# Time mixing: small key, receptance and state products moved between and behind the large ones, one state sum per chunk, two state buffers

## The reference, cut to what matters

```python
xrkv = x[None] + xx[None] * mu[:3, None, None, :]
r, k, v = jnp.einsum('nbsd,nde->nbse', xrkv, w_rkv)
decay = jnp.exp(-jnp.exp(w_log.astype(f32)))
a = jax.nn.sigmoid(a0 + (xa @ a1) @ a2)
g = jax.nn.sigmoid(xg @ g1) @ g2
kk = kk / jnp.maximum(jnp.sqrt(jnp.sum(kk * kk, axis=-1, keepdims=True)), 1e-12)
k = k * (1 + (a - 1) * k_a)
bh = kk * ah

def step(state, inp):
    r_t, w_t, k_t, v_t, kk_t, b_t = inp
    sa = jnp.einsum('bhvk,bhk->bhv', state, -kk_t)
    state = (state * w_t[:, :, None, :] + sa[..., None] * b_t[:, :, None, :]
             + v_t[..., None] * k_t[:, :, None, :])
    return state, jnp.einsum('bhvk,bhk->bhv', state, r_t)
```

## Time and profile before

| | us |
|---|---|
| median of 3 runs | 1254.25 (1253.86 to 1259.63) |
| the profiled execution's own time | 1260.84 |
| its span | 1259.1 |
| PE busy | 1143.4 (91%) |
| DVE busy | 933.9 (74%) |
| ACT busy | 555.9 (44%) |
| mean granted PE clock | 0.943 |

### The profile page before, as it was taken

One profiled execution on the slowest core, in us unless ns is written; L12 is line 12 of the kernel. 1 busy time (PEld: TensorE's weight loads), 2 busy tenths in 40 slices (PEclk: granted clock), 3 DMA queues, 4 the chain that ended last, 5 costly groups with the idle time before them and its releaser, 6 DMA issues.

```text
span 1259.1 us, 20232 instructions
## 1 busy us (share of the span) xinstructions
PE 1143.4 (91%) x7950; PEld 914.9 (73%) x7950; DVE 933.9 (74%) x1242; ACT 555.9 (44%) x797; POOL 9.7 (1%) x27
## 2 busy tenths in 40 slices
PE   5899999898689999999999997888978877999998
PEld 1678888776467788877788885666758865888886
DVE  4888888688967988878888886887880876644453
ACT  2454444455844444355445435493232213543331
POOL 2000000000000000000000000000000000000000
PEclk8999999899799999999999998889976788999999
DMA  9889887373229789866888893125321112655540
GB/s 328 285 286 321 304 292 263 134 267 69 67 68 347 273 294 321 309 227 232 288 299 299 291 348 115 50 85 168 124 67 38 51 54 99 201 170 199 200 167 34
DMA packets 185852, 252.88 MB, mean 201 GB/s; under 512 B 30449, under 2 KB 121585, under 8 KB 185777
## 3 DMA queue, kind: packets, MB, share of 16 engines
q1 hardware_dynamic: 181554, 251.32, 59.0%
q10 hardware_dynamic: 4224, 0.52, 0.3%
HBM read 249.71 MB, written 2.10 MB: 200 GB/s over the span
## 4 chain that ended last, share of the span: by engine, by line
PE 69%; DVE 17%; DMA 5%; issue 4%; ACT 4%; SPq 0%; POOL 0%; DVEq 0%; ACTq 0%; POOLq 0%
PE bank L725 20%; PE bank L727 19%; PE bank L726 19%; DVE ada_acc L1839 4%; DVE gu_lo L1911 3%; DMA last_raw<-in_ffn_w_down_dram 2%; DVE dn_lo L1921 1%; DMA front<-in_ada_w_dram 1%; ACT gu_hi L1334 1%; PE bank L1200 1%; PE bank L787 1%; PE bank L1085 1%; DMA ada_raw<-in_ada_w_dram 1%; PE bank L734 1%; DVE probs L2453 1%
## 5 line engine op out<-in xcount | busy, mean ns | idle before, releaser
L725 PE MATMUL bank<-gu_hi,xT_hi 128*128 128x512 f32 (+1 forms) x944 | 375.4, 398 | 22.4 <-DVE gu_lo L1911 9.1
L726 PE MATMUL bank<-gu_lo,xT_hi 128*128 128x512 f32 (+1 forms) x944 | 371.9, 394 | 0.0
L727 PE MATMUL bank<-gu_hi,xT_lo 128*128 128x512 f32 (+1 forms) x944 | 371.7, 394 | 0.0
L1911 DVE TENSOR_TENSOR gu_lo<-raw,gu_hi 128x2048 fp32r<-128x2048 f32 (+1 forms) x108 | 239.8, 2252 | 15.3 <-ACT gu_hi L1334 14.9
L725 PEld LDWEIGHTS bank<-gu_hi,xT_hi 128*128 128x128 f32 x944 | 180.9, 192 | 66.5 <-issue 17.5
L726 PEld LDWEIGHTS bank<-gu_lo,xT_hi 128*128 128x128 f32 x944 | 180.8, 192 | 38.7 <-issue 0.7
L727 PEld LDWEIGHTS bank<-gu_hi,xT_lo 128*128 128x128 f32 x944 | 180.7, 191 | 38.0
L1334 ACT CAST gu_hi<-raw 128x2048 fp32r<-128x2048 f32 (+1 forms) x108 | 200.2, 1883 | 13.8 <-DMA raw<-in_ffn_w_gu_dram 10.0
L1839 DVE SCALAR_TENSOR_TENSOR ada_acc<-ada_raw,cact,ada_acc 128x512 f32<-128x512 f32 x224 | 168.4, 752 | 11.1 <-DMA ada_raw<-in_ada_w_dram 1.2
L725 PE MATMUL bank<-dn_hi,hT_hi 128*128 128x512 f32 x320 | 132.6, 414 | 1.8 <-DVE dn_lo L1921 1.8
L1921 DVE TENSOR_TENSOR dn_lo<-raw,dn_hi 128x2048 fp32r<-128x2048 f32 x40 | 91.6, 2290 | 53.0 <-ACT dn_hi L1345 53.0
(11 more groups left out here) (285 smaller groups left out, 1176.0 us busy)
## 6 DMA issues: line engine op xcount, KB each, us to landing
raw<-in_ffn_w_gu_dram SPq DMA_DIRECT2D x176, 512.0 KB, 8.4
ada_raw<-in_ada_w_dram SPq DMA_DIRECT2D x128, 512.0 KB, 7.1
raw<-in_ffn_w_down_dram SPq DMA_DIRECT2D x40, 1024.0 KB, 5.0
raw<-in_rwkv_w_rkv_dram SPq DMA_DIRECT2D x24, 512.0 KB, 5.0
raw<-in_dsa_w_in_dram SPq DMA_DIRECT2D x16, 512.0 KB, 4.5
front<-in_ada_w_dram SPq DMA_DIRECT2D x8, 512.0 KB, 7.8
last_raw<-in_ffn_w_down_dram SPq DMA_DIRECT2D x4, 1024.0 KB, 8.2
raw<-in_dsa_w_out_dram SPq DMA_DIRECT2D x8, 512.0 KB, 4.9
```

The lines of the kernel that those rows point to most:

```text
L725: nc.tensor.matmul(out_ap, sta_hi, mov_hi, start=start, stop=False, skip_group_check=True)
L726: nc.tensor.matmul(out_ap, sta_hi, mov_lo, start=False, stop=False, skip_group_check=True)
L727: return nc.tensor.matmul(out_ap, sta_lo, mov_hi, start=False, stop=stop, skip_group_check=True)
L1911: nc.vector.tensor_tensor(gu_lo[:, par, ks, 0:width], buf[:, i, 0:4 * width].rearrange("p (k c) -> p k c", k=4), gu_hi[:, par, ks, 0:width ...
```

## The change

On PE, `ak` becomes a stream: after each large product (three passes) of `V_BLOCK+1` eight of its matmuls are issued, 16 times. `pairs` too: 16 matmuls behind each of the last six groups of transposes, and 20 behind each of the 8 products for g. The 12 groups of transposes are spread: two ahead of and two behind the second half of `R_BLOCK+1`, two behind `turn_r(1)`. The seven key-value products leave their place; in the recurrence each goes into the bank of the b-by-U product, between WT*S and the wait for U, and the b-by-U product is summed onto it there. The product with rT moves behind the product with U. S has two buffers.

On DVE `b_to_end` is gone: the sum of S and the bank is multiplied by the chunk's decay (two instructions in a row after `s_mm`, in place of two ahead of it and one behind). `r_scaled(0)` and `(1)` go behind steps 22 and 25 (from 26 and 29). `rest_of_mix(MIX_R)` is halved: its first half ahead of the 31 steps. `late_start` and one rest of output weights go ahead of the recurrence; the other pieces are cut in two and put around the wait for `s_mm`, and the last quarter of the rests goes behind the recurrence.

On ACT `round_mix(MIX_R)`'s first half waits only for the first half of `V_BLOCK+1` (`half_done`), and comes with `round_half(R_BLOCK, 1)` ahead of the copies of v. The seven copies of `kv` are gone. On SP the load of `R_BLOCK`'s second half goes ahead of the wait for the stored matrices and the load of `inv_in`.

```diff
             # SP
+                load_half(R_BLOCK, w_r, 0, 1)
                 sp.wait_ge(inv_saved, 8 * 16)
                 sp.dma_start(inv_in[:].rearrange("p s u -> p (s u)"), inv_dram[0]).then_inc(inv_loaded, 16)
-                load_half(R_BLOCK, w_r, 0, 1)
             # PE
+                            if also is not None:
+                                some(also, 8)
+                def some(stream, n):
+                    for _ in range(n):
+                        next(stream, None)
-                project(V_BLOCK + 1, 0, bank[2:4])
-                project(V_BLOCK + 1, 1, bank[2:4])
-                ak()
+                ak_stream = ak()
+                project(V_BLOCK + 1, 0, bank[2:4], also=ak_stream)
+                project(V_BLOCK + 1, 1, bank[2:4], also=ak_stream)
-                srcs = [negT, kdT, b_end]
+                srcs = [negT, kdT, bT]
+                turn_tok(0)
+                turn_tok(1)
+                project(R_BLOCK + 1, 1, bank[2:4])
+                turn_tok(2)
+                turn_tok(3)
+                turn_r(1)
+                turn_tok(4)
+                turn_tok(5)
                 pe.wait_ge(r_ready, 2)
-                pairs(0, G)
-                pairs(1, bank[2:4])
+                pairs_stream = itertools.chain(pairs(0, G), pairs(1, bank[2:4]))
+                for i in range(6, 12):
+                    turn_tok(i)
+                    some(pairs_stream, 16)
...
+                        nc.tensor.matmul(ring[2 * t + d][:], hid_g[:, 0, ts], g2[:, 0, ds], start=True, stop=False)
+                        some(pairs_stream, 20)
...
+                        some(pairs_stream, 20)
-                for c in range(NC - 1):
-                    if c < 4:
-                        pe.wait_ge(g_out, c + 1)
-                    else:
-                        pe.wait_ge(kv_out, c - 3)
-                    state_update(c, kd_tok, v_tok, ring[c % 4]).then_inc(kv_mm, 1)
             # PE, in the recurrence, behind WT by S
+                    if c < NC - 1:
+                        state_update(c, kd_tok, v_tok, bank[2], True)
+                    pe.wait_ge(u_ready, 2 * c + 2)
+                    if c < NC - 1:
+                        state_update(c, b_tok, U, bank[2], False).then_inc(s_mm, 1)
+                    if c:
                         for j in range(KD):
                             for e in range(2):
                                 nc.tensor.matmul(ys[t][e][rows, j * HD:(j + 1) * HD], rT[half_of(e), j, ts],
-                                                 S[half_of(e), j, :], start=False, stop=True,
+                                                 S[c % 2][half_of(e), j, :], start=False, stop=True,
             # DVE
-                    elif n == 22:
-                        b_to_end()
-                    elif n == 26:
+                    elif n == 22:
                         r_scaled(0)
-                    elif n == 29:
+                    elif n == 25:
                         r_scaled(1)
+                late_start(0)
+                late_start(1)
+                rest_of_block(RWKV_OUT0, 1, halves=range(1, 2))
...
                     if c < NC - 1:
-                        added = kv[:, c, :].rearrange("p (j c) -> p j c", c=HD)
-                        dve.wait_ge(kv_out, c + 1)
+                        added = bank[2][:].rearrange("p (j c) -> p j c", c=HD)
+                        dve.wait_ge(s_mm, c + 1)
                         if c:
-                            chain(nc.vector.tensor_tensor(S_part[:], S[:], added, ALU.add))
+                            chain(nc.vector.tensor_tensor(S_part[:], S[c % 2][:], added, ALU.add))
                             added = S_part[:]
-                        chain(nc.vector.tensor_tensor(S_part[:], added, chunk_decay[:, :, c:c + 1].broadcast_to([P, KD, HD]),
-                                                      ALU.mult))
-                        dve.wait_ge(s_mm, c + 1)
-                        nc.vector.tensor_tensor(S[:], S_part[:], bank[2][:].rearrange("p (j c) -> p j c", c=HD), ALU.add
+                        nc.vector.tensor_tensor(S[(c + 1) % 2][:], added,
+                                                chunk_decay[:, :, c:c + 1].broadcast_to([P, KD, HD]), ALU.mult
                                                 ).then_inc(s_ready, 1)
             # DVE, behind the recurrence, ahead of rest_of_y(0)
+                rest_quarter(1, 2)
             # ACT
-                for c in range(NC - 1):
-                    act.wait_ge(kv_mm, c + 1)
-                    nc.scalar.copy(kv[:, c, :], ring[c % 4][:]).then_inc(kv_out, 1)
```

More of the change, by code:

```diff
@@ L1 @@
+import itertools
 from contextlib import ExitStack
@@ L1148, in rwkv, with turn_tok @@
                 turn_r(0)
-                project(R_BLOCK + 1, 1, bank[2:4])
-                turn_r(1)
-                srcs = [negT, kdT, b_end]
+                srcs = [negT, kdT, bT]
                 ring = TB + bank[0:2]
-                for i in range(12):
+                def turn_tok(i):
                     what, t, d = i // 4, i // 2 % 2, i % 2
@@ L1165, in rwkv @@
                     mm.then_inc(turned, 1)
[L1166 to L1172, removed]
-                        mm = nc.tensor.matmul(ring[2 * t + d][:], hid_g[0:GL - P, 1, ts], g2[0:GL - P, 1, ds],
-                                              start=False, stop=True)
-                        mm.then_inc(g_ready_rwkv, 1)
+                turn_tok(0)
[6 more added lines that the diff above has]
+                turn_tok(5)
                 def pairs(t, into):
@@ L1540, in round_half, with round_mix @@
                                    ).then_inc(hi_ready[i], 1)
[L1542 to L1548 removed]
+                def round_mix(m, halves=range(2)):
+                    for half in halves:
+                        ks = slice(4 * half, 4 * half + 4)
+                        act.wait_ge(mix_ready, KD + (1, 4, 5)[m])
+                        if m != MIX_K:
+                            if half == 0:
+                                act.wait_ge(half_done, 2 * m)
+                            else:
+                                act.wait_ge(g_ready[1], K_BLOCK + 2 * m)
                         nc.scalar.copy(xT_hi[:, ks, :], mixes[m][:, ks, :]).then_inc(mix_hi_ready, 1)
@@ L1649, in rwkv, with tok @@
                 x1_to_U(1, bank[0:2])
-                act.wait_ge(turned, 10)
-                projected(R_BLOCK + 1, bank[2:4], lambda t: r_tok[:, t, :])
                 ring = TB + bank[0:2]
                 dsts = [a_tok, kd_tok, b_tok]
-                for i in range(12):
+                def tok(i, after):
                     what, t, d = i // 4, i // 2 % 2, i % 2
-                    act.wait_ge(turned, 12 + i + 1)
+                    act.wait_ge(turned, after + i + 1)
                     nc.scalar.copy(dsts[what][:, t, d * HALF:(d + 1) * HALF], ring[i % 4][:]).then_inc(tok_out, 1)
-                round_block(RWKV_OUT0, 1, free=True, halves=range(0, 1))
+                act.wait_ge(turned, 10)
+                tok(0, 10)
+                tok(1, 10)
+                projected(R_BLOCK + 1, bank[2:4], lambda t: r_tok[:, t, :])
+                tok(2, 10)
+                tok(3, 10)
+                for i in range(4, 12):
+                    tok(i, 12)
                 for t in range(TT):
@@ L1714, in rwkv @@
                                            ).then_inc(y_out, 1)
-                        round_block(RWKV_OUT0 + 1, 0, free=True, halves=range(1, 2))
                     elif c == 5:
@@ L1718, in rwkv @@
                     elif c == 6:
+                        round_block(RWKV_OUT0 + 1, 0, free=True, halves=range(1, 2))
                         y_root(0)
@@ L2018, in mix_in, with rest_of_mix @@
                             ins.then_inc(mix_ready, 1)
-                def rest_of_mix(m):
-                    for half in range(2):
+                def rest_of_mix(m, halves=range(2)):
+                    for half in halves:
                         ks = slice(4 * half, 4 * half + 4)
```

146 lines of the change are left out of this document (79 added, 67 removed).

## The result

The change made the kernel faster by a third of what was forecast. Seven runs of each: 1254.25 us before, 1248.28 us after (1243.95 to 1250.88), so -6.0 us as medians; the ratio is 0.9931 [0.9913, 0.9949], or -8.7 us, as three of the seven before were long (1258.4 to 1262.0). Two later comparisons gave 0.9947 and 0.9945, -6.4 and -7.2 us as medians. Forecast were 1234.5 us and -19.8.

What follows compares the result with a forecast made beforehand. PE bounds the kernel (91% busy), with little to win outside the mixing, and DVE bounds the recurrence; u0(0) 24.6 us earlier, recurrence +4.8, sum -19.8: 1254.25 to 1234.5 us. Forecast range 1230 to 1239 (0.51), 8 in 10 within 1226 to 1246.

Steps and rivals of the forecast that it cites:

- ak among V_BLOCK+1: In V_BLOCK+1: each group of eight ak matmuls costs 0.38 us, 16 groups 6.1 us, ending at 880.1.
- Operands of R, DVE's steps: Ahead of pairs: inv_in 2.4 us late, DVE's 31 steps from 876.2 to 928.5 instead of 933.2, r_scaled(1) ending at 912.5.
- pairs: Handed out among transposes and g products: 19.1 us at clock 1.00, from 912.5 to 931.6, where it ended at 940.2.
- Rival 2: Gaps stay with small matmuls in V_BLOCK+1 and pairs: 12 us less gain, 1246.5 (1240 if only the first part); chance 0.17.
- Rival 3: Clock falls inside pairs, transposes and g double (+11), gain only 8.8: 1245.5; chance 0.10.
- Key-value products, outputs, bonus: Ahead of u0(0): 12.7 us of products gone, outputs 3.6 to 2.0, bonus 6.92 to 5.2; u0(0) 24.6 us earlier, at 938.8.
- The inverse's way back: Ahead of u0: the inverse's store and loads finish at 936.9 instead of 941.5, with cover of 1.9 us.
- The recurrence (+4.8): From u0 to the output projection: +1.3 first product, +1.3 six chunks, +1.0 head means, +1.2 last quarter of rests.
- my +1.3 for the six chunks: Recurrence, U of chunk 1 to chunk 7: PE busy 31 of 38 us, with 7.7 more full at 39.
- Rival 4: PE at half clock from pairs through the recurrence, 1.8 us per 16 matmuls, +14.7 in all: 1269; chance 0.04.
- Rival 1: The recurrence gets shorter, PE at full clock with a chunk's chain of 5.2 us: 1228; chance 0.13.
- The signs of being wrong: Issue gap in V_BLOCK+1; PE clock under 0.7 (913-932); PE waiting for inv before u0; U copies under 34/over 43 us apart.

Runs made afterwards that it cites:

- experiment 2: The changed kernel with the 128 matmuls of ak in a row behind V_BLOCK+1 again: 1246.52 us, 0.9924 of the kernel before.
- experiments 2 and 3: The changed kernel with, in the first, ak's 128 matmuls in a row, and in the second, pairs' 256 in a row: 1246.52 and 1256.7 us.
- c2: The changed kernel, unchanged, profiled once more: 0.9947 of the kernel before.
- c3: The changed kernel, unchanged, one more profile: 1248.82 us.
- f1: The changed kernel, unchanged, timed again in five rounds: 1248.48 us, 0.9945 of the kernel before.
- e6: The changed kernel with twelve large passes of zeros in a row ahead of WT*S of chunk 1: 1245.75 us, 0.9928 of the kernel before.
- e7: The changed kernel with twelve passes of zero weights but v as moving values ahead of WT*S of chunk 1: 1245.4 us, 0.9922 of the kernel before.
- e9: The changed kernel with twelve passes of zeros in three groups of four, up to WT*S of chunk 1: 1245.19 us, 0.9913 of the kernel before.
- e11: As e9, with ak in a row: 1245.56 us, 0.9917 of the kernel before.
- e10: The changed kernel with key-value products ahead of the recurrence and rT*S ahead of the wait for U: 1248.41 us, 0.9936 of the kernel before.
- e2: The changed kernel with pairs' 256 matmuls in a row (the second of experiments 2 and 3): 1256.7 us, 1.0018 of the kernel before.

## Why the prediction was wrong, by its steps

- **ak among V_BLOCK+1** (0.38 us a group, end 880.1): right within a us. A group's period is 1.12 us, 0.43 more than its three passes, so 6.9 us for 16 in place of 6.1; the end came at 879.61 because this execution began `ba` 1.2 us earlier. That it earns nothing, since DVE's steps are the bound at `pairs`, was in the text only as "up to 1.7 us lost in V_BLOCK+1 cost nothing"; experiment 2 puts all of the hand-out in that class.
- **Operands of R, DVE's steps** (start 876.2, `r_scaled(1)` 912.5, end 928.5): 876.80, 913.5, 929.3. Right. (The text says "six rests" and names five; its sum is that of five.)
- **pairs** (912.5 to 931.6): PE waited 2.98 us for DVE, then ran to 931.93, at clock 1.00. Rival 2 (the gaps stay) is refuted: no issue gap in L1075, and the gaps come back in a row (experiments 2 and 3). But gaps remain in other runs of small matmuls: 0.9 to 2.3 us in `wt(0)` in all five profiles of the changed kernel, and 0.4 to 2.8 us in the key-value product of chunk 5. Rival 3's 11 us did not come; the clock did stand at 0.50 for 3.4 to 6.8 us around the start of `pairs` in c2, c3 and f1. That the gaps are the loading of instructions fits all this but no run isolates it. If they are, the "mostly hidden" of the Trainium skill (Runtime: NRT & Kernel Launch, "Instruction fetch mechanics") is contradicted in this case for small matmuls in a row, with idle times of 1.3 to 7.3 us, and agrees for large ones.
- **Key-value products, outputs, bonus** (`u0(0)` 24.6 us earlier): 963.28 to 938.65, 24.6. That it agrees to the tenth is luck: 1.2 us of it lie ahead of `ba`, where nothing was changed. Against the start of `ba` the three profiles of before average 114.7 us, not 116.0, as the bonus took 6.92 us in the one used and 4.1 and 3.8 in the others; the first profile after has 92.6 where the mean is 93.7. The usual gain is 21.0, so the term is 3.6 us large as a mean. The bonus forecast at 5.2 was 4.2 to 6.7. The inverse's way back was not late.
- **The recurrence (+4.8): the step that failed.** It came out at +8.8 in the first pair of profiles and +11.0 in the mean: +3.5 up to W1 (forecast 1.3), +6.2 from W1 to W7 (forecast 2.3, with the head means), +1.3 behind (forecast 1.2). I summed each added product at 1.3 us, set PE's 39 us of work against a stretch of 38, and left the clock as it was, 0.83. The busy time came near (39.22 us), though my 31 of 38 us was a wider stretch than the 36.3 of the earlier trace rows with PE's 29.17. But the chunks differ: chunks 1 and 2, at 1.92 us a product and clock 0.50, have PE full for 9.15 us each, with nothing to take from, while from chunk 3 on the clock is mostly 1.0 and PE has idle time. The sum over the stretch hid that. With the clock up (e6, e7, e9, e11) W1 to W7 is 33.0 to 34.7 us, 2 to 4 below the kernel before, and my +1.3 for the six chunks would have been too much. So the work was priced well enough at the old clock, and what the products cost at half of it was left out. Of the +3.5 up to W1, the first product and gaps called "issue" explain part; no experiment was made on it.
- **Rival 4** named the mechanism, PE at half clock with 1.8 us a product (measured 1.92), and gave it 0.04, for the clock of the whole stage; it happened for chunks 1, 2 and the start of 3. My ground against it, that the old kernel had clocks of 0.75 and 0.83 with less PE work, failed: the small matmuls of these chunks run at 0.50 with PE busy 100% of the time. Rival 1 (1228) has its chunk of 5.2 us (measured 5.08) only where the clock is up.
- **The signs of being wrong** did not come: no issue gap in `V_BLOCK+1`, a clock near 1.0 in `pairs`, PE over 90% busy in the recurrence, and 41.0 us between the U copies of chunks 1 and 7, inside 34 to 43. None of them asked for the clock of single chunks.
- **The balance.** Of the 13.8 us between forecast and timed medians, 6.2 are the recurrence, 3.6 the stretch ahead of `u0`, 0.4 lies outside the stage, and 3.6 stand between the profiled mean (-9.6) and the medians (-6.0). The last part stays open.

What stays open: what decides when the clock rises. It rose 0.2 to 2.0 us into chunk 3, behind the 32x32 products of chunk 2, in all five profiles of the changed kernel, and at the end of the twelve passes in both profiles with them (964.7 and 964.6). Also open is the difference between profiled and timed gain, as said above.

## What to carry to other kernels

Before work is moved off a full engine onto one with slack, look at that engine's granted clock where the work will land, slice by slice: with PE's old share of work half clock in two chunks left the stretch at 37 us (e10), and with the added products the same clock was worth 9 us. Spread runs of over a hundred small matmuls among large ones where they are on the path (8 us here in the timed runs), and don't bother where another engine sets the next start (0 us). An order that fills a wait is worth having once; a second filler for the same wait adds nothing. And take the profile that a forecast starts from more than once: the one used here had 3 us more in the bonus than its two repetitions.

## What the runs showed of the hardware

- PE busy for all of 20.40 us with small fp32 matmuls on 64x32, 32x64 and 32x32 tiles stayed at 1.2 GHz but for the last 0.1 us. The Trainium skill (TensorE: Matmul & The Clock Gate, "What's actually happening") says that "the default state is throttled, and activity releases the throttle"; a PE that the profile shows as fully busy wasn't released for 20 us here. It was at the end of twelve 128x512 passes, 5.4 us (e6, e7), with zeros as with values moving.
- A product of 16 such matmuls is 1.08 to 1.15 us at 2.4 GHz and 1.92 to 1.97 at 1.2 GHz, with its weight loads: at half the clock they take 1.7 to 1.8 times as long.
- 256 small matmuls in a row and the 64 behind them show idle times of 1.82, 1.91 and 1.30 us in which PE waits for no semaphore (e2); with transposes and large products between them there is none in the changed kernel.
